# An expert layer whose outputs are finished inside the last expert that each token visits

## The reference, cut to what matters

```python
probs  = softmax(x @ w_router + b_router)          # 16 experts in 4 groups of 4
gsel   = argmax over groups of the sum of the group's two best probs
vals, idx = top_k(where(in_group, probs, -1), 2)   # two experts, both of the chosen group
wts    = vals / sum(vals)
moe    = sum over the two experts: wts * (silu(x @ w_gate) * (x @ w_up)) @ w_down
y      = LN(ALPHA * x + moe) * ln2_g + ln2_b
```

## Time and profile before

| | us |
|---|---|
| median of 3 runs | 906.55 (906.45 to 909.16) |
| the profiled execution, its own time | 905.72 |
| its span in the profile | 904.5 |
| TensorE (PE) busy | 870.0 |
| VectorE (DVE) busy | 360.6 |
| ScalarE (ACT) busy | 206.3 |
| GpSimd (POOL) busy | 84.3 |

### The profile page before, as it was taken

The page is one execution under the profiler, slowest core; times in us unless marked ns, Lnnn a source line. Parts: engine busy times, 40 slices in busy tenths (PEclk is TensorE's granted clock), DMA queues, the critical chain, the costliest instruction groups (busy, mean ns, idle before and its releaser), DMA issues.

```text
span 904.5 us, 20975 instructions
## 1 busy us (share of the span) xinstructions
PE 870.0 (96%) x9437; PEld 712.3 (79%) x9437; DVE 360.6 (40%) x749; ACT 206.3 (23%) x313; POOL 84.3 (9%) x89
## 2 busy tenths in 40 slices
PE   7999999999999999999999999699999999999965
PEld 6999888898989999999999988566666565655631
DVE  5653645636575471233232446612311111111146
ACT  4521141311522232322222102131101110110112
POOL 1210000000000001000101011401000100100043
PEclk9999999999999999999999999899999999999988
DMA  9895171491816043221222914999999999999357
GB/s 324 263 287 149 47 276 51 160 311 49 279 47 209 1 155 94 93 88 53 95 93 70 400 73 177 337 362 384 382 393 407 408 393 411 411 387 416 126 165 169
DMA packets 85374, 203.47 MB, mean 225 GB/s; under 512 B 4237, under 2 KB 57189, under 8 KB 76472
## 3 DMA queue, kind: packets, MB, share of 16 engines
q1 hardware_dynamic: 78216, 177.17, 53.9%
q0 software_dynamic: 7088, 25.26, 9.0%
HBM read 172.58 MB, written 32.06 MB: 226 GB/s over the span
## 4 chain that ended last, share of the span: by engine, by line
PE 93%; DMA 3%; DVE 2%; ACT 1%; issue 1%; POOL 0%; SPq 0%; DVEq 0%; POOLq 0%; ACTq 0%
PE psum L2158 19%; PE psum L465 17%; PE psum L467 16%; PE psum L466 16%; PE psum L2172 9%; PE psum L1862 2%; PE psum L2145 2%; PE psum L1872 2%; PE psum L1901 1%; DMA xg<-x_rows,idx_i 1%; PE psum L2104 1%; PE psum L2071 1%; PE psum L1887 1%; PE psum L2036 1%; PE psum L2178 1%; DMA y_slots<-ys 1%
## 5 line engine op out<-in xcount | busy, mean ns | idle before, releaser
L465 PE MATMUL psum<-x_hi,split_lo 128*128 128x272 f32 x704 | 208.8, 297 | 2.0 <-DVE pbl L1426 1.2
L467 PE MATMUL psum<-x_hi,split_hi 128*128 128x272 f32 x704 | 202.3, 287 | 0.0
L466 PE MATMUL psum<-x_lo,split_hi 128*128 128x272 f32 x704 | 202.2, 287 | 0.0
L2158 PE MATMUL psum<-set,xt 128*32 128x256 f32 x3072 | 169.1, 380 | 0.0
L2158 PEld LDWEIGHTS psum<-set,xt 128*32 128x32 f32 x3072 | 98.2, 110 | 65.7 <-issue 2.4
L465 PEld LDWEIGHTS psum<-x_hi,split_lo 128*128 128x128 f32 x704 | 132.7, 188 | 7.3 <-issue 2.7
L466 PEld LDWEIGHTS psum<-x_lo,split_hi 128*128 128x128 f32 x704 | 132.8, 189 | 1.4 <-issue 1.0
L467 PEld LDWEIGHTS psum<-x_hi,split_hi 128*128 128x128 f32 x704 | 132.6, 188 | 0.0
L460 DVE TENSOR_TENSOR split_lo<-raw,split_hi 128x2048 fp32r<-128x2048 f32 x35 | 80.0, 2290 | 113.8 <-ACT split_hi L441 113.3
L2172 PE MATMUL psum<-set,hT 128*32 128x256 f32 x1536 | 86.2, 380 | 1.5 <-DVE ys L1650 1.5
L2172 PEld LDWEIGHTS psum<-set,hT 128*32 128x32 f32 x1536 | 49.0, 110 | 32.8 <-ACT hT L1050 1.7
(11 more groups left out here) (355 smaller groups left out, 1253.4 us busy)
## 6 DMA issues: line engine op xcount, KB each, us to landing
set<-in_w_e_gate_dram SPq DMA_DIRECT2D x32, 1024.0 KB, 10.4
set<-in_w_e_up_dram SPq DMA_DIRECT2D x32, 1024.0 KB, 12.8
set<-in_w_e_down_dram SPq DMA_DIRECT2D x32, 1024.0 KB, 12.6
raw<-in_w_in_dram SPq DMA_DIRECT2D x26, 1024.0 KB, 6.0
cb<-in_state_C_dram SPq DMA_DIRECT2D x8, 1024.0 KB, 7.6
out_dram<-cb SPq DMA_DIRECT2D x8, 1024.0 KB, 5.8
y_slots<-ys POOLq DMA_DIRECT2D x15, 384.0 KB, 6.4
y_slots<-x_hi POOLq DMA_DIRECT2D x3, 1536.0 KB, 14.8
```

Source lines behind the costliest of these rows:

```text
L465: nc.tensor.matmul(out, a_lo, b_hi, start=first, stop=False)
L466: nc.tensor.matmul(out, a_hi, b_lo, start=False, stop=False)
L467: return nc.tensor.matmul(out, a_hi, b_hi, start=False, stop=last)
L2158: last = mm(gate_up()[32 * b:32 * b + 32, j], xt[:, kk, 32 * mine:32 * mine + 32], w, start=kk == 0 and j != 1, stop=kk == KT - 1 and j > 0)
```

## The change

- **Order.** The n-th turn works on expert `EXP[n]` = 0, 4, 8, 12, 1, 5, 9, 13, 2, ...: first the four experts of rank 0 in their groups, then rank 1, and so on. Of a token's two experts the one of lower rank is thus done at least four turns earlier.
- **Finish in the slots of the second expert.** From turn 4 on, each turn gathers for its slots the result rows of the tokens' first expert from a DRAM tensor per group, `y_group` (POOL, `gather_first`); scales the gathered rows of x1 by ALPHA (ACT, `scaled_rows`); adds the first result, weighted (DVE, `add_first`); and, a turn later, adds this expert's result, takes the norm and writes the rows by two indirect DMAs to the prompt's and the sample's outputs (`finish` on DVE, `store_final` on POOL). Slots whose token has this expert as its first get an index beyond the bounds, and nothing is moved for them.
- **Buffers.** Four buffers for gathered rows in place of two; two each for the first results and for the sums (`sums_`). `scaled_rows(n)` waits until the two DMAs of `store_final(n - 2)` have landed.
- **Indices.** Each token's two weights, its first slot and its second expert go to DRAM (`pick_rows`) and are gathered by slot, four experts at a time (`gather_picks` in POOL's turns 1, 5 and 9); `slot_targets` on DVE works out the indices.
- **Start.** SP waits for the first gather to land before it loads the weights of turn 1; the second norm's parameters come after the first reloads. All one-hot groups after the second hold four experts.
- **Gone.** The tail after the last expert, the bias written into the outputs, and the zeros in `y_slots`. The branch for extra blocks now holds a general path of its own, which gathers both results for all tokens.
- **Loops** over the turns are written out on SP, ACT and DVE; PE loops over ranks 1 and 2.

```diff
-OH_FIRST = (0, 1, 4, 7, 10, 13, NE)
+OH_FIRST = (0, 1, 4, 8, 12, NE)
+EXP = [(n % EG) * EG + n // EG for n in range(NE)]
+FIN0 = EG
+SKIP = 4096.0
...
+    pick_rows = nc.dram_tensor("pick_rows", [N, 4], F32).ap()
+    y_group = [nc.dram_tensor(f"y_group{q}", [(EG - 1) * CAP, DM], F32).ap() for q in range(NE // EG)]
...
+    xg2, xg3, yf0, yf1, sum0 = lay(r_xt, r_xt + NT * DM * 4, *[(n, [P, DM], F32) for n in ("xg2", "xg3", "yf0", "yf1", "sum0")])
...
+    xg, ys, yf, sums_, sets = (xg0, xg1, xg2, xg3), (ys0, ys1), (yf0, yf1), (sum0, sum1), (set0, set1)
...
-            if h == 1:
-                for i in range(PT):
-                    sp.dma_start(y_prompt[0, i * P:(i + 1) * P, :], ln2_b[0].partition_broadcast(P)).then_inc(bias_out, 16)
-                sp.dma_start(y_sample.rearrange("b t d -> (b t) d"), ln2_b[0].partition_broadcast(NS)
-                             ).then_inc(bias_out, 16)
...
         sp.wait_ge(z_done, J_WO)
-        sp.wait_ge(y_out, 16 * (XTRA // 4))
-        sp.wait_ge(y15_out, 16)
...
         store_rows()
+        sp.wait_ge(g_in[0], 16)
+        for half in range(2):
+            load_gate_up(EXP[1], 1, half)
+        for half in range(2):
+            load_down(EXP[1], 1, half)
+        store_prompt_states(0, 3)
+        reload_gate_up(EXP[2], 0, 1)
+        store_prompt_states(3, H)
+        reload_gate_up(EXP[3], 1, 3)
+        reload_down(EXP[2], 0, 1)
         sp.wait_ge(x1_out, 16 * NT)
+        sp.wait_ge(cp_out, 16 * H)
+        sp.wait_ge(np_ok, 1)
         sp.dma_start(lng[:], ln2_g[0].partition_broadcast(P)).then_inc(ln_in, 16)
-        for half in range(2):
...
-        reload_down(2, 0, 1)
-        with sp.Fori(2, NE // 2) as t:
-            reload_gate_up(2 * t, 0, 4 * t - 3)
...
+        sp.dma_start(lnb[:], ln2_b[0].partition_broadcast(P)).then_inc(ln_in, 16)
+        for n in range(4, NE):
+            reload_gate_up(EXP[n], n % 2, 2 * n - 3)
+            reload_down(EXP[n - 1], (n - 1) % 2, 2 * n - 5)
+        reload_down(EXP[NE - 1], 1, 2 * NE - 3 - 2)
...
-        pl.wait_ge(y15_out, 16)
+        def gather(n):
+            idx = bass.IndirectOffsetOnAxis(ap=idx_i[0:CAP, n:n + 1].bitcast(U32), axis=0)
+            pl.indirect_dma_start(xg[n % 4][0:CAP], None, x1_rows, idx).then_inc(g_in[n % 4], 16)
...
+        def store_y(n):
+            pl.wait_ge(ya_ok, n + 1)
+            pl.wait_ge(yd_ok, n + 1)
+            r, q = divmod(n, EG)
+            dst = y_group[q][r * CAP:(r + 1) * CAP] if r < EG - 1 else y_slots[EXP[n] * CAP:(EXP[n] + 1) * CAP, :]
+            pl.dma_start(dst, ys[n % 2][0:CAP]).then_inc(ys_out[n % 2], 16)
+        def gather_picks(r):
+            for n in range(4 * r, 4 * r + 4):
+                idx = bass.IndirectOffsetOnAxis(ap=idx_i[0:CAP, n:n + 1].bitcast(U32), axis=0)
+                pl.indirect_dma_start(pk[0:CAP, n, :], None, pick_rows, idx).then_inc(pk_in, 16)
+        def gather_first(n):
+            pl.wait_ge(slots_ok, n // 4)
+            pl.wait_ge(ys_out[n % 2], 16 * ((n - FIN0) // 2 + 1))
+            if n >= FIN0 + 2:
+                pl.wait_ge(first_ok, n - FIN0 - 1)
+            idx = bass.IndirectOffsetOnAxis(ap=from_i[0:CAP, n:n + 1].bitcast(U32), axis=0)
+            pl.indirect_dma_start(yf[n % 2][0:CAP], None, y_group[n % EG][0:n // EG * CAP], idx,
+                                  bounds_check=n // EG * CAP - 1, oob_is_err=False).then_inc(yf_in[n % 2], 16)
+        def store_final(n):
+            q = n % 4
+            pl.wait_ge(fv_ok, n - FIN0 + 1)
+            nc.gpsimd.tensor_tensor(hrs[0:CAP, q:q + 1], hve[0:CAP, q:q + 1], minus_half[0:CAP, 0:1], ALU.pow
+                                    ).then_inc(fr_ok, 1)
+            pl.wait_ge(fin_ok, n - FIN0 + 1)
+            for rows, idx, most in ((y_prompt.rearrange("o t d -> (o t) d"), to_p, SEQ - 1),
...
+                at = bass.IndirectOffsetOnAxis(ap=idx[0:CAP, n:n + 1].bitcast(U32), axis=0)
+                pl.indirect_dma_start(rows, at, sums_[n % 2][0:CAP], None, bounds_check=most, oob_is_err=False
+                                      ).then_inc(fin_out[n % 2], 16)
         pl.wait_ge(idx_ok, 1)
         pl.wait_ge(x1_out, 16 * NT)
         pl.wait_ge(ps_done, 2)
         gather(0)
         pl.wait_ge(idx_ok, 2)
-        gather(1)
-        pl.wait_ge(y_out, 16 * (XTRA // 4))
-        for e in range(2, NE):
-            if e in OH_FIRST:
-                pl.wait_ge(idx_ok, OH_FIRST.index(e) + 1)
-            pl.wait_ge(xt_done, e - 1)
-            gather(e)
-            if e >= 4:
-                store_y(e - 4)
-        for e in range(NE - 4, NE - 1):
-            store_y(e)
+        for n in range(1, 4):
+            gather(n)
+        pl.wait_ge(idx_ok, 3)
+        pl.wait_ge(xt_done, 1)
+        gather(4)
+        for n in range(1, NE):
+            store_y(n - 1)
+            if n + 4 < NE:
+                if (n + 4) % 4 == 0:
+                    pl.wait_ge(idx_ok, (n + 4) // 4 + 2)
+                pl.wait_ge(xt_done, n + 1)
+                if n >= FIN0:
+                    pl.wait_ge(xs_ok, n - FIN0 + 1)
+                gather(n + 4)
+            if n == 1:
+                pl.wait_ge(pick_ok, 1)
+                pl.dma_start(pick_rows[0:SEQ].rearrange("(i p) c -> p i c", p=P), pick[:, 0:PT, :]).then_inc(pick_out, 16)
+                pl.dma_start(pick_rows[SEQ:N], pick[0:NS, PT, :]).then_inc(pick_out, 16)
+                pl.wait_ge(pick_out, 32)
+            if n % 4 == 1 and n + 3 < NE:
+                gather_picks((n + 3) // 4)
+            if FIN0 <= n + 1 < NE:
+                gather_first(n + 1)
+            if n - 1 >= FIN0:
+                store_final(n - 1)
...
+        store_final(NE - 1)
         hold()
...
-        def gather_rows(a, buf, i):
-            r = ROWS[i]
-            idx = bass.IndirectOffsetOnAxis(ap=dest_i[0:r, a, i:i + 1].bitcast(U32), axis=0)
-            pl.indirect_dma_start(buf[i][0:r], None, y_slots, idx).then_inc((ya_in, yb_in)[a][i], 16)
...
-            r = ROWS[i]
-            nc.scalar.mul(x1[0:r, i, :], x1[0:r, i, :], ALPHA).then_inc(xal_ok, 1)
...
+        def scaled_rows(n):
+            if n >= FIN0 + 2:
+                ac.wait_ge(fin_out[n % 2], 32 * ((n - FIN0) // 2))
+            nc.scalar.mul(sums_[n % 2][0:CAP], xg[n % 4][0:CAP], ALPHA).then_inc(xs_ok, 1)
+        for n in range(1, NE):
+            gate_sigmoid(2 * n + 2)
+            if n < NE - 1:
+                columns(n + 2)
+            if n >= FIN0:
+                scaled_rows(n)
+            if n >= 3:
+                ac.wait_ge(ys_out[(n - 1) % 2], 16 * ((n - 1) // 2))
+            if n - 3 >= FIN0:
+                ac.wait_ge(both_ok, n - 3 - FIN0 + 1)
+            store_half(n - 1, 2 * n)
+            hidden_columns(n + 1)
         ac.wait_ge(ys_out[1], 16 * (NE // 2 - 1))
-        store_half(1, 2 * NE)
+        ac.wait_ge(both_ok, NE - 2 - FIN0)
+        store_half(NE - 1, 2 * NE)
...
-        for i in range(NT):
-            r = ROWS[i]
-            nc.scalar.activation(diag[0:r, i, 0:r], const("ident", r)[:, 0:r], ACT.Copy, scale=gates_ab[0:r, 1, i:i + 1]
-                                 ).then_inc(dg_ok, 1)
...
+            step(choice(lg[:], bc(const("expert"), 1, [P, NT, NE]), rk[:], ALU.mult))
+            step(v.tensor_reduce(pick[:, :, 3:4].rearrange("p i o -> p (i o)"), lg[:], AX.X, ALU.add))
...
+            v.tensor_copy(pick[:, :, 2:3].rearrange("p i o -> p (i o)"), dest_f[:, 0, :]).then_inc(pick_ok, 1)
...
         silu(0)
+        rows_of(2)
         choice_gates()
...
         extra_blocks()
...
         result_rows()
...
+        def slot_targets(r):
+            at = slice(4 * r, 4 * r + 4)
...
+            v.tensor_scalar(past[0:CAP, at], tokf[0:CAP, at], SEQ - 0.5, 2 * SKIP, ALU.is_lt, ALU.mult)
+            ve_.wait_ge(pk_in, 64 * r)
...
+                                   ).then_inc(slots_ok, 1)
+        def add_first(n):
+            ve_.wait_ge(xs_ok, n - FIN0 + 1)
+            ve_.wait_ge(yf_in[n % 2], 16 * ((n - FIN0) // 2 + 1))
+            acc = sums_[n % 2][0:CAP]
+            v.scalar_tensor_tensor(acc, yf[n % 2][0:CAP], pk[0:CAP, n, 0:1], acc, ALU.mult, ALU.add).then_inc(first_ok, 1)
+        def finish(n):
+            q, acc = n % 4, sums_[n % 2][0:CAP]
+            ve_.wait_ge(first_ok, n - FIN0 + 1)
+            ve_.wait_ge(ya_ok, n + 1)
+            ve_.wait_ge(yd_ok, n + 1)
+            v.scalar_tensor_tensor(acc, ys[n % 2][0:CAP], pk[0:CAP, n, 1:2], acc, ALU.mult, ALU.add).then_inc(both_ok, 1)
+            ve_.wait_ge(both_ok, n - FIN0 + 1)
+            for b in range(2):
+                last = v.bn_stats(lst[0:CAP, q, b, :], acc[:, 512 * b:512 * b + 512])
+            step(last)
+            step(v.bn_aggr(hmv[0:CAP, q, :], lst[0:CAP, q].rearrange("p q s -> p (q s)")))
+            v.tensor_scalar(hve[0:CAP, q:q + 1], hmv[0:CAP, q, 1:2], EPS, None, ALU.add).then_inc(fv_ok, 1)
+            step(v.scalar_tensor_tensor(acc, acc, hmv[0:CAP, q, 0:1], lng[0:CAP], ALU.subtract, ALU.mult))
```

(50 more changed lines are left out.)

286 lines of the change are left out of this document (91 added, 195 removed).

## The result

The changed kernel takes 925.06 us (median of 4 runs, 923.35 to 930.88) against 906.5 us: a ratio of 1.0217, 95% interval 1.0173 to 1.0261. It is slower, by some 19 us where 11 less were forecast, and outside the forecast's range of 877 to 917. The profiled execution took 924.68 us, 923.5 of them span.

What follows compares the result with a forecast made beforehand. TensorE was taken as the bound, busy 870.0 of 904.5 us, so time could come only from its gaps or the tail. -21.2 - 6.6 + 17.0 = -10.8 gave 895.8 us against the median; range 877 to 917.

Steps and rivals of the forecast that it cites:

- the tail: After PE's last matmul: 35.4 us replaced by copies, finish, two issues and a landing, 14.2 us; -21.2 us.
- The start: Before turn 1: expert 1's loads held until the first gather lands, PE waits 0.4 us instead of 5.5; -6.6 us.
- the start gives nothing: Rival at the first gather: DVE's one-hot products held it, not the loads; 902.4 us, chance 0.08 by itself.
- The turns: Turns from 4 on: rounds of waits of 18.1 us against PE's 17.36 make PE stall; +17.0 us.
- the slower rival: Turns 7 to 15: rounds of 19.3 us or more; 919 us if scatters land in 9.0; chance 0.22, both forms.
- its other form: Beside finish: POOL's issues held behind one DVE instruction of 1.28 us; round 19.4, time 907 us, within the 0.22.
- the ring: Turns from 4 on: scaling, first result, copies, finish, scatters, landing (6.4 us), next scaling; one round 18.1 us.
- Lateness: Time by which scaled_rows(n) ends after PE's turn n; over 6.7 us PE stalls, 5.0 in turn 10, 7.5 in sum.
- Loops at nothing: Loops over the turns: written out, they cost nothing on engines that mostly wait.
- The picks at nothing: POOL's turn 1: writing and gathering picks up to the last landing takes 25 us, leaving 6 us of cover; no cost.
- Bytes at nothing: DMA per turn: 18.1 us at 411 GB/s, 0.8 too many, but weights have 17 us of cover; no cost.
- all covered: Rival in the turns: landing under 5.5 us makes the round under 17.2, shorter than a turn; 878.8 us, chance 0.27.

Runs made afterwards that it cites:

- the first two experiments: Changed kernel with four sum buffers instead of two: 899.87 us; changed kernel with PE's loop written out, two sum buffers kept: 921.34 us.

## Why the prediction was wrong

**What bounds the kernel, and the tail.** Right: 12.5 us from the last matmul against 14.2 forecast. `finish(15)` took its 6 us; the last scatter's issue at 921.15 is 2.35 us from the end of the span, where I had 5; no weights were under way.

**The start.** Right in its cause, too large in its worth: the first gather landed 5.8 us after its issue (570.25 to 576.1; forecast 5.2), PE waited 0.33 for it. Turn 1 starts 4.5 us earlier and not 6.6, because turn 0 now waits 0.86 us for the second gather's 17.65 us and its gate and up take longer (10.99 instead of 10.57). Held loads alone moved turn 1 by 5.2 us in the kernel before, and its time by 6.0. The rival "the start gives nothing" is out.

**The turns, the step that failed first.** The mechanism, its order and its small pieces were right; the landing was mis-sized. I took 6.4 because it was the nearest row by kind, a write from SBUF. It was 9.3 to 11.2 in the rounds from 721 to 848 us, nearer to the 9.0 of the gathers, which were nearer in another way: indirect, row by row, behind the same neighbours. With 0.84 us to the issue, where I had 0.1, the round is 22 instead of 18.1. That is the slower rival (a landing of 9.0, time 919), in which I put 0.22 with its other form. The other form, POOL's issues held beside DVE, is not what happened: no issue of a scatter in any round took over 1.00 us, and none of a gather in the round above over 0.97, against 0.94 before. The rule of the Trainium skill on shared access ("SBUF — State Buffer", "Who interferes with whom") is about an instruction of GpSimd that reads SBUF, and the trace bears it out for the root alone: 1.12 to 1.14 us or 1.54 beside DVE's centring, 0.57 and 0.59 in the two rounds in which the picks had put it behind the centring (at 698.12 and 789.95 us). The prediction stretched it to the issues, which the section doesn't say. The skill's fit for a transfer of 384 KB, an estimate of 2.9 us ("DMA: Bandwidth & Descriptors", "Anatomy of one DMA — SWDGE (gpsimd) path"), is near the last landing of the chain, 2.77 us for a part of the 96 rows, after the weights are through, and by 4 us or more below every one among them. Mending the ring alone gave 25 us back.

**Lateness.** I let PE stall for DVE from turn 10 on, by 5.0 us there. It did, and turn 10 took 6.6 us more than before, though the rounds were longer than I took them: PE had lost 12 us to its own stops in turns 6 to 8, and the ring ran on under them. The 46.4 us are: turns 1 to 3, 2.0 more than before; turn 6, 4.4; turns 7 and 8, 8.1; longer gate and up in turns 4 and 5, 0.6; turns 9 to 14, 24.0, the ring with the low clock behind its stalls; from turn 15's start to the last matmul 7.3, with a wait of 6.46 for DVE, where I had 8.0. So the ring shows as some 31 us, with the loop and the picks at 14 beside it, and 1.0 for the larger one-hot products in turns 1 and 2. Those, at nothing in my sum, would have put the time near 911 even if the turns had cost the 17.0 that I gave the ring (an estimate).

**Loops at nothing, wrong.** I wrote that written-out loops cost nothing "on engines that mostly wait". PE doesn't wait, and its loop grew to four turns. The jump back costs 6.3 us and 2.9 us of slow matmuls in the kernel before (11.0 us of time), 4.6 and 3.1 in the changed one, of which the ring hid half: writing PE out gave 3.7 there.

**The picks at nothing, wrong in another place.** I had priced their path (25 us, cover 31) and not what 384 packets of 16 bytes do to others. Moving them moved PE's stops from turns 6 and 10 to turn 4, and no trace of a kernel without them has such stops. They aren't the only cause: with the scatters ahead of the gathers, four indirect DMAs of rows issued within 5 us have shorter stops with them. By what way such DMAs hold up PE no run shows. Why the profiled executions of the first two experiments show no such stops, with the same picks, is open, as is why gate and up takes about 11.0 instead of 10.57 for many turns in some executions (0.4 us a turn; with picks and without).

**Bytes at nothing, wrong.** The 7.45 MB a turn were not what failed; the rate was. The 411 GB/s of the earlier trace rows were one turn's; over the ten turns from 654.3 to 827.8 us the kernel before moved 402, the changed one 378, and the six kernels with four sum buffers that compute everything 378 to 384, at a full DMA share. The change adds indirect rows and packets to every turn; the picks alone are not it, since without their gathers the rate is 381. Which of the rest takes it, no run isolates. By estimate turns then need 7.45 / 0.384 = 19.4 us of the DMA engines, 2.0 over PE, 24 us in twelve turns against 17 of cover. In the changed kernel the ring hid that; every kernel without the ring met it. Six of them, mended in different ways, lie between 896.6 and 899.9 us, and only moving less (887.8) went below. So the rival "all covered", 878.8, was not to be had by mending the ring: it needed a rate that no kernel with this change reached.

Of the kernels that compute everything, the fastest has four sum buffers, PE written out and empty slots skipped: 896.64 us, with an interval that overlaps those of four others. But one added wait in the kernel before gives 899.97, some 60% of that gain by the ratios.

## What to carry to other kernels

When a buffer waits for a scatter to land, price the landing by a transfer of the same form (indirect, among the same loads), and take enough buffers that the ring isn't near the length of a turn. A change that removes work from the end and puts it beside a full DMA stage must be costed by that stage's rate with the new packets in it, not by the old rate. And for an engine without idle time the size of a loop's body is a cost of its own.
